# A fused token-mixer and mixture-of-experts layer on one core: which expert weights are loaded, split and waited for where the layer turns into its experts

## The reference

```python
h = modulate(rmsnorm(x, norm_mix_g), sh_m, sc_m)      # sh_m, sc_m: columns of silu(c) @ w_ada + b_ada
z = h @ w_in                                          # 5120 columns; the first ones computed are those of v
...                                                   # gating, pooling, two branches
x = x + g_m * (merged @ w_out)
hf = modulate(rmsnorm(x, norm_ffn_g), sh_f, sc_f)
# 16 experts in 4 groups, top 2 of the best group
g = einsum('td,edf->tef', hf, w_gate)                 # w_gate, w_up: 16 x 1024 x 512
u = einsum('td,edf->tef', hf, w_up)
a = silu(g) * u * combine
y = einsum('tef,efd->td', a, w_down)                  # 16 x 512 x 1024
out = rmsnorm(x + g_f * y, final_norm_g)
```

## Time and profile before

| | |
|---|---|
| three executions | 767.85, 770.69, 770.92 us (median 770.69) |
| the profiled execution, its time | 770.69 us |
| its span, first to last instruction | 768.8 us |
| TensorE busy | 743.4 us (97%) |
| VectorE busy | 599.6 us (78%) |
| ScalarE busy | 392.2 us (51%) |
| GpSimd busy | 195.8 us (25%) |
| moved by DMA | 187.18 MB, mean 243 GB/s |
| mean granted TensorE clock | 0.995 of full |

### The profile page before, as it was taken

The page is one execution under the profiler, slowest core; times in us unless marked ns, Lnnn a source line. Parts: engine busy times, 40 slices in busy tenths (PEclk is TensorE's granted clock), DMA queues, the critical chain, the costliest instruction groups (busy, mean ns, idle before and its releaser), DMA issues.

```text
span 768.8 us, 10951 instructions
## 1 busy us (share of the span) xinstructions
PE 743.4 (97%) x3500; PEld 612.6 (80%) x3501; DVE 599.6 (78%) x824; ACT 392.2 (51%) x360; POOL 195.8 (25%) x80
## 2 busy tenths in 40 slices
PE   7899999999999999999999899999999999999995
PEld 6788888776888888887788587888888888888884
DVE  4894426764674765758768899999999999999985
ACT  4546333324232231324345267777777777777744
POOL 1000004102000000000064111555555555555533
PEclk9999999999999999999999999999999999999999
DMA  8989414211375563917472818899999999999895
GB/s 299 318 271 389 151 55 147 72 56 57 109 267 170 167 215 123 313 55 273 170 265 85 318 44 294 308 370 393 365 366 364 363 358 384 373 369 374 313 187 168
DMA packets 108709, 187.18 MB, mean 243 GB/s; under 512 B 7096, under 2 KB 58360, under 8 KB 108685
## 3 DMA queue, kind: packets, MB, share of 16 engines
q1 hardware_dynamic: 101276, 173.58, 62.7%
q0 software_dynamic: 5792, 11.65, 5.6%
q10 hardware_dynamic: 1616, 1.65, 0.6%
HBM read 180.47 MB, written 15.73 MB: 255 GB/s over the span
## 4 chain that ended last, share of the span: by engine, by line
PE 85%; DVE 8%; DMA 3%; issue 1%; ACT 1%; SPq 1%; DVEq 0%; POOLq 0%; ACTq 0%
PE ps L1522 25%; PE ps L1523 25%; PE ps L1524 25%; DVE wsplit L843 3%; PE ps L1782 2%; DMA raw<-in_w_ada 2%; PE ps L1886 1%; PE ps L1652 1%; DVE raw L932 1%; PE ps L1713 1%; DMA raw<-in_w_out 1%; DMA work<-hf_rows,tok_idx 1%; PE ps L1818 1%; PE ps L1772 1%; DVE raw L886 1%
## 5 line engine op out<-in xcount | busy, mean ns | idle before, releaser
L843 DVE TENSOR_TENSOR wsplit<-raw,wsplit 128x2048 fp32r<-128x2048 f32 x128 | 289.8, 2289 | 57.0 <-ACT wsplit L565 34.2
L752 ACT ACTIVATE wsplit<-raw 128x2048 fp32r<-128x2048 f32 x96 | 183.8, 1921 | 69.4 <-PE ps L1524 69.4
L512 POOL DMA_INDIRECT expert_rows<-work,dest_now x14 | 106.8, 7628 | 105.2 <-DVE work L1402 97.3
L1522 PE MATMUL ps<-wsplit,hgT 128*128 128x512 f32 x264 | 104.5, 396 | 1.3 <-DVE hgT L1313 1.3
L1524 PE MATMUL ps<-wsplit,hgT 128*128 128x512 f32 x264 | 103.1, 390 | 0.0
L1523 PE MATMUL ps<-wsplit,hgT 128*128 128x512 f32 x264 | 102.9, 390 | 0.0
L1522 PE MATMUL ps<-hT,wsplit 128*128 128x512 f32 x256 | 101.1, 395 | 1.0 <-DVE mx L1028 1.0
L1524 PE MATMUL ps<-hT,wsplit 128*128 128x512 f32 x256 | 99.7, 390 | 0.0
L1523 PE MATMUL ps<-hT,wsplit 128*128 128x512 f32 x256 | 99.7, 390 | 0.0
L886 DVE SCALAR_TENSOR_TENSOR raw<-raw,c_silu 128x256 f32 (+1 forms) x128 | 62.0, 485 | 12.6 <-DMA raw<-in_w_ada 8.6
L520 POOL TENSOR_TENSOR wsplit<-raw,wsplit 128x2048 fp32r<-128x2048 f32 x2 | 9.2, 4614 | 198.3 <-ACT wsplit L565 198.2
(11 more groups left out here) (299 smaller groups left out, 1278.3 us busy)
## 6 DMA issues: line engine op xcount, KB each, us to landing
raw<-in_w_exp_gate SPq DMA_DIRECT2D x32, 1024.0 KB
raw<-in_w_exp_up SPq DMA_DIRECT2D x32, 1024.0 KB
raw<-in_w_exp_down SPq DMA_DIRECT2D x32, 1024.0 KB
raw<-in_w_in SPq DMA_DIRECT2D x20, 1024.0 KB
raw<-in_w_ada SPq DMA_DIRECT2D x16, 1024.0 KB
raw<-in_w_ada SPq DMA_DIRECT2D x16, 512.0 KB, 5.9
expert_rows<-tmp SPq DMA_DIRECT2D x4, 1024.0 KB, 11.4
raw<-in_w_branch_a SPq DMA_DIRECT2D x4, 1024.0 KB
```

The costliest lines, as they stand in the source:

```text
L512: g.indirect_dma_start(out=y_dram, out_offset=bass.IndirectOffsetOnAxis(ap=dest_now[:, 0:1], axis=0), in_=y, in_offset=None, bounds_check= ...
L752: A_(wsplit[:, c, 0, :], raw[:, c, :], ACT.Copy).then_inc(hi_ready, 1)
L843: V.tensor_tensor(wsplit[:, n, 1, :], raw[:, slot, :], wsplit[:, n, 0, :].bitcast(F32), ALU.subtract).then_inc(lo_ready, 1)
L1522: nc.tensor.matmul(out, w_hi, m_hi_, start=first, stop=False)
```

## The change

It touches three places.

1. **Weights at the turn.** Slots 2 and 3 of `raw`, once expert 0's gate is split, take expert 1's up weights. Expert 0's up weights now go to slots 4 and 5 after hf is stored, ahead of the first gate half of expert 1; expert 0's down weights follow in the same slots 4 and 5, each half after the low part of the up half before it. So ScalarE copies M0 + 2 and M0 + 3 together, after the two copies of the output gain, and VectorE makes the low part of M0 + 2 after the tile counts and of M0 + 3 after `select(2)`. The counts in `hi_c` follow. The last chunk of `w_out` goes to `wsplit` slot 4 in place of 5.
2. **VectorE's order around tile 0.** Two steps on the tile table (`r_le`, `r_n`) move from before `indices(1)` to behind the first tile's token split. The split of chunk 0 moves behind `select(2)`, and `indices(2)` from behind `rows_lo(1)` to behind that split.
3. **TensorE's head.** 5 unread products in place of 8 after the first column sums; `mod_columns(1)` after six pairs of the k = 1 round in place of four; the 5 unread products before the next block are gone.

```diff
         def split_slot(n):
             if n == M0 - 1:
-                return 5
+                return 4
...
             for c in range(2):
                 sp.wait_ge(lo_ready, M0 + 1 + c)
-                load(c + 2, w_up[0, :, 4 * c:4 * c + 4, :], 4)
+                load(c + 2, w_up[1, :, 4 * c:4 * c + 4, :], 4)
...
             sp.wait_ge(hf_saved, 16 * NT)
+            for c in range(2):
+                load(c + 4, w_up[0, :, 4 * c:4 * c + 4, :], 4)
             load(0, w_gate[1, :, 0:4, :], 4)
             for c in range(2):
+                sp.wait_ge(lo_ready, M0 + 3 + c)
                 load(c + 4, w_down[0, :, 2 * c:2 * c + 2, :], 2)
-            for c in range(2):
-                sp.wait_ge(lo_ready, M0 + 3 + c)
-                load(c + 2, w_up[1, :, 4 * c:4 * c + 4, :], 4)
...
-                if t == 0:
-                    hi(split_slot(M0 + 2), 2, 16 * (RAW_O // 4 + 3), G0 + 16)
             for t in range(2, NT):
                 turned(act, A_, t)
-            hi(split_slot(M0 + 3), 3, 16 * (RAW_O // 4 + 3), M0)
             act.wait_ge(sub_ready, 1)
...
+            for c in range(2):
+                hi(c + 4, c + 4, 16, M0)
...
-                    act.wait_ge(landed[c], (i + (2, 2, 4, 4, 1, 1)[c] + (11 if c < 4 else 0)) * 16)
+                    act.wait_ge(landed[c], (i + (2, 2, 3, 3, 2, 2)[c] + (11 if c < 4 else 0)) * 16)
...
-                if t == NT - 1:
-                    dve.wait_ge(lo_ready, M0 + 2)
-                    lo_n(M0 + 2, 2)
                 mixed(t, 1)
...
-            lo_n(M0 + 3, 3)
-            step(V.tensor_tensor(r_le, iota1[:, 0:TILES_MAX].unsqueeze(2).broadcast_to(ie),
-                                 r_cum.unsqueeze(1).broadcast_to(ie), ALU.is_gt))
-            done()
-            step(V.tensor_reduce(r_n, r_le, AX_X, ALU.add))
-            done()
+            lo_n(M0 + 2, 4)
             indices(1)
...
+            step(V.tensor_tensor(r_le, iota1[:, 0:TILES_MAX].unsqueeze(2).broadcast_to(ie),
+                                 r_cum.unsqueeze(1).broadcast_to(ie), ALU.is_gt))
+            done()
+            step(V.tensor_reduce(r_n, r_le, AX_X, ALU.add))
+            done()
...
-            dve.wait_ge(hi_ready, M0 + 5)
-            lo(0, 0)
             select(2, expert_ahead(0))
+            lo_n(M0 + 3, 5)
...
                 if prev:
                     select(i + 2, e2)
-                    lo_c(0)
+                lo_c(0)
+                if not prev:
+                    indices(i + 2)
                 lo_c(1)
                 if not prev:
                     rows_lo(i + 1)
-                    indices(i + 2)
...
-            idle_products(8, 6, 0)
+            idle_products(5, 6, 0)
...
-                    if k == 1 and i == 4:
+                    if k == 1 and i == 6:
                         mod_columns(1)
...
-                if q == 1:
-                    pe.wait_ge(gain_ready, 2)
-                    idle_products(5, MOD_BANK, P)
```

## The result

| | before | after |
|---|---|---|
| median of the runs, us | 770.51 (767.39 to 771.32, 8 runs) | 775.6 (774.05 to 777.02, 8 runs) |
| ratio after / before | | 1.0077 (95%: 1.0059 to 1.0093) |
| profiled execution: time, span | 770.69, 768.8 | 774.07, 772.1 |
| mean granted clock of TensorE in it | 0.995 | 0.991 |

The change costs 5.1 us where 0.9 was forecast, and the time lies outside the range of 768.8 to 774.2. The predicted +0.9 was a balance of a shorter DMA wait, a longer VectorE chain and one fall of the clock. The gain at the gather was forecast 1.3 us too large and the growth of VectorE's chain 0.6 us too small, and the head of the program, to which the prediction gave 0.1 us, costs 3.5 in the profiled execution.

A forecast was written before the change was run, and what follows sets the result against it. TensorE was taken as busy nearly throughout, VectorE as the bound from the gather's landing to tile 2. From 770.69, turn -0.74 and head +0.1, together -0.6, gave 770.0; a clock fall of +1.6 gave 771.6. Range 768.8 to 774.2.

The forecast's parts named there:

- Part 1: Head: fewer unread products cost 0, later second column sums delay the next weight block; +0.1 us.
- waits of 0.7 to 1.3 us there left the clock whole: Head: the argument against a clock fall at the 2.3 us gap before the second weight block.
- a rival of +1.6: Head: the clock falls at the 2.3 us gap, +1.6 us, giving 773.2; chance 0.10.
- Part 2: Layer end: taking the weight split out before the last residual gains 0, as it was hidden all but 0.05 us.
- Part 3: First gather: one load less queued ahead, so it lands 2.45 us earlier, in 4.4 us for 6.86.
- Part 4: VectorE from gather to tile 2: split +2.2, table steps +1.14, idle times -1.78, index wait +0.15; with the gather -0.74 us.
- the -1.78 for the three idle times: VectorE's chain into tile 2: its waits of 0.54, 0.79 and 0.45 us on TensorE or its follower vanish.
- the 0.15: VectorE's chain into tile 2: what is left of waiting, for the third index product; +0.15 us.
- Part 5: Before tile 2: TensorE waits 3.2 us and the clock falls to 1.2 GHz, likelier than not; +1.6 us.
- The other fall: Behind the first gather: half clock, about 1.6 us, said not to move the end before, only make VectorE's three idle times.
- The rival "gather no earlier": First gather still lands after 435, VectorE's chain pays the whole price: 773.8, or 775.4 with the clock fall; chance 0.17.
- VectorE's split: At 431.99, 2.29 us, while the first gather runs: unchanged after, named as support for the gather landing no earlier.

The follow-up runs named there:

- e16: The whole change with unread products filling each TensorE wait it makes or lengthens, 8 again behind the first column sums: 771.96 us, ratio 1.003.
- e3: The kernel before with 5 unread products in place of 8 behind the first column sums, nothing else: 769.89 us, ratio 0.9999.
- e14: The changed kernel itself, run once more for a second trace: 777.3 us.
- e11: The kernel before with the second column sums two blocks later and no unread products before the second weight block: 772.06 us, ratio 1.0024.
- e1: The kernel before with the change's three head edits and nothing else: 773.4 us, ratio 1.0054.
- e7: The kernel before with expert 1's up loads both waiting for the fourth split, so three loads, not four, precede the first gather: 769.65 us, ratio 0.9991.
- e2: The changed kernel with its three head edits undone: 772.54 us, ratio 1.003.
- e8: The kernel before with 16 unread products in place of 6 ahead of the first gather's wait: 768.62 us, ratio 0.9981.
- e6: The changed kernel with the head of before and the second gate half's split put before the third selection on VectorE: 770.55 us, ratio 1.0004.
- e17: e13 with 5 unread products put into TensorE's wait before the first column sums: 770.01 us, ratio 1.0006.
- e4: The kernel before without the 5 unread products ahead of the second weight block, nothing else: 769.72 us, ratio 0.9987.
- e10: e1 with nine unread products in the 2 us wait before the second weight block: 771.86 us, ratio 1.0033.
- e15: The changed kernel with the head of before and 12 unread products in TensorE's wait before tile 2: 770.86 us, ratio 1.0017.
- e13: The kernel before with the edits of e4, e8 and e7 together: 768.19 us, ratio 0.9981.

## Why the prediction was wrong

**Part 1, the head: the step on the clock failed.** The order's share was forecast at +0.1 and measured at +0.15 (e16, clock whole, with the wait filled and 8 products behind the first sums); the wait was forecast at 2.3 us and is 2.03. What failed is the sentence "waits of 0.7 to 1.3 us there left the clock whole", and the chance of 0.10 made from it. It compared a 2 us wait with shorter ones, gave the loss of three fillers 0 because they only lengthen a wait (0.81 us to 1.48 in e3), and did not ask what the fillers were for. All three edits act on it: behind the first fall, that 12 of 18 profiles have and the profiled execution of before did not, 5 products do not bring the clock back before the weight blocks; the later sums without fillers leave the 2 us wait, behind which three of four profiles with it fell (after, e14, e11; not e1). Measured: +3.5 and +4.0 us in the two traces of after, against a rival of +1.6. How the three edits share this isn't settled: e3 alone shows the longer fall in its trace and no loss in its times.

**Part 2** held: the residual at the layer's end waits 2.08 us for TensorE, with nothing behind it later for that.

**Part 3, the gather: a term mis-sized.** The mechanism is right, and e7 shows it in both directions, for the first gather and for the second. The size was 2.45 us and is 1.13 (6.86 to 5.73; 5.50 in e2). The 4.4 of the earlier trace rows was taken from a gather that met an empty queue. This one still met the end of three loads: in 429.4 to 433.5 the load queue of after moved 1.60 MB, and TensorE's wait is 1.93 us, not 0.6.

**Part 4, VectorE's chain: a term missing.** The terms named came true: one more split, the table steps behind the token split, the three waits gone, no wait for the third index product. They summed to +1.71; the chain grew by 2.35. And the -1.78 for the three idle times holds only against an execution that has the fall behind the gather: at full clock (e8) 0.62 us of them are left, 0.16 before the indices and 0.46 before the product of gate and up. The last is the one that the prediction took for a wait on TensorE; its row says "issue", and it is as long at full clock. Missing was the register read of 1.07 us, which in before lay beside the split `lo(0, 0)`. The change put the selection ahead of the splits, and the prediction followed the instructions but not the register read between them. e6 moves the read behind a split again: its chain is 0.8 us shorter, and its time can't be told from before's. With 1.07 added and the 0.15 left out the sum is 2.63; the rest of 0.28 is that instructions without a wait between them overlap by about 0.09 us, at the three places where a wait went (two splits in a row take 4.49, one 2.29).

**Part 5, the clock before tile 2: the right mechanism, in part of the executions only, and mis-sized.** The wait was forecast at 3.2 us and is 2.9. Of the four profiles that have it (after, e14, e2, e6) one fell. Where it falls it costs 2.8 us, not 1.6: the fall lasts from the wait to 481.7, some 6 us of products, where the earlier trace rows and its neighbours made me count nine products.

**The other fall**, behind the gather, was counted as harmless: it "only made VectorE's three idle times". Turns of 51.6 with it and 50.4 without show that it costs 1.2 us here; in e11, where it lasted twice as long (435.6 to 442.2), the turn is 2.4 us longer, and in e1 3.0, with a gather 0.7 us later. Those idle times were on the path to tile 2, as the prediction's own sum in part 4 says; the two sentences contradict each other.

**The rival "gather no earlier"** did not happen. It gave a time of 773.8 to 775.4 near the measured one, but for a reason that the trace refutes. The Trainium skill, DMA: Bandwidth & Descriptors, section Queues, rings and completion order, would have the gather's packets take turns with the loads'; e7 speaks against it here: 4.9 or 6.86 us with three or four loads ahead, 4.4 or 7.8 with little or two loads ahead. Nor is it VectorE's split, which the prediction named beside it: in e7 the packets moved while that split ran (431.04, 2.29 us).

**The sum again**, for after against before at their profiled executions: head +3.5, of it 0.15 order; 0.24 between; turn +1.2 (gather and what leads to it -1.14, chain +2.35), which is +2.4 for the order less the 1.2 of before's fall at the gather; nothing or +2.8 behind tile 2; less 1.67 for an earlier start. Medians differ by 5.1. The base was a second error: the one profiled execution of before lay at the median by two faults that cancel, a start that was over 1 us later than in nearly all other profiles and a head without the fall.

## What to carry to other kernels

Unread products on TensorE are not dead weight: before taking them out or moving work over them, ask which wait they fill and whether the granted clock was whole behind it, in more than one execution where it can be had; but none belong in front of work that is ready (e17). Before work is moved on an engine's queue, follow the register reads too: the 1.07 us of "issue" showed in after and not in before or e6, where a split runs beside the read. And a gather was here as late as the loads queued ahead of it: moving loads away from the first one put them in front of the second.

## What the runs showed of the hardware

- The same wait doesn't always have the same end. Behind 3.1 us before the gathered tokens the clock fell in before, e4, e10 and e11 and stayed whole in e3. Behind 1.93 us the clock stayed whole in after, behind 1.94 and 1.95 us it fell in e15 and e14; behind 2.9 us it stayed three times and fell once. The mean clock of an execution says how much it lost to falls: the executions of after lie between 0.982 and 0.992.
- One fall cost 1.2 to 2.8 us where TensorE, or an engine that waited for it, set the time, by how much dense work followed at 1.2 GHz; the first fall of the head cost next to nothing where 8 unread products took it up (heads of 33.72 to 34.21 in e4, e13, e6 and e2, for 33.91 without), but 1.3 us in e15, where it lasted to 26.9. At 1.2 GHz two weight products start 0.42 us apart (476.26 to 476.68), at full clock 0.23.
- The gather's packets wait for the loads queued ahead of it: from issue to landing 6.86 to 7.62 us with four loads of 1 MB ahead, 4.7 to 5.75 with three, 4.2 to 4.5 with a nearly empty queue, 6.8 to 7.8 with two issued just ahead.
- The start varies by up to 1.6 us between executions: the first column sums start between 18.64 and 20.27 in 16 of 18 profiles, and at 21.17 in that of before (the last is e17, with products ahead of them).
